# Convolution taps moved into the first projection of a hybrid diffusion trunk on Trainium2

## What is computed

```python
def _conv_module(u2, p):
    a, b = jnp.split(u2, 2, axis=-1)
    u = a * jax.nn.sigmoid(b)
    y = lax.conv_general_dilated(u, p['conv_w'][:, None, :].astype(u.dtype), window_strides=(1,),
                                 padding=((CONV_WIDTH // 2, CONV_WIDTH // 2),),
                                 dimension_numbers=('NWC', 'WIO', 'NWC'), feature_group_count=CONV_DIM)
    y = jax.nn.silu(_layer_norm(y + p['conv_b'], p['conv_ln_g'], p['conv_ln_b']))
    return y @ p['w_conv_out']
...
def _mixing(h, p, kv_ctx):
    ...
    u2, q, k, v, f, g = jnp.split(h @ p['w_in'], SPLITS, axis=-1)
    ...
    conv_out = _conv_module(u2, p)
    ...
    merged = gates[:, :, 0] * conv_out + gates[:, :, 1] * attn_out + gates[:, :, 2] * fnet_out
    return merged @ p['w_out'], k, v
```

## Time and profile before

| | |
|---|---|
| median of 3 runs | 1402.83 us (1402.35 to 1403.17) |
| the profiled execution | 1399.74 us, of which the span of the trace is 1397.9 us |
| PE busy | 1262.8 us (90%) |
| DVE busy | 914.3 us (65%) |
| ACT busy | 619.3 us (44%) |
| POOL busy | 300.6 us (22%) |
| attention's first scores on PE | 311.49 us from the span's start |

### The profile page before, as it was taken

One profiled execution on the slowest core, in us unless ns is written; L12 is line 12 of the kernel. 1 busy time (PEld: TensorE's weight loads), 2 busy tenths in 40 slices (PEclk: granted clock), 3 DMA queues, 4 the chain that ended last, 5 costly groups with the idle time before them and its releaser, 6 DMA issues.

```text
span 1397.9 us, 18848 instructions
## 1 busy us (share of the span) xinstructions
PE 1262.8 (90%) x7338; PEld 1009.5 (72%) x7338; DVE 914.3 (65%) x1070; ACT 619.3 (44%) x693; POOL 300.6 (22%) x199
## 2 busy tenths in 40 slices
PE   2899979997999999999798459999999999999992
PEld 1688769985888999999797436666666666666661
DVE  1501656779766233613745549999999999999993
ACT  2421122221433222231212237777777777777772
POOL 1051000000332222233221402222222222222212
PEclk9899989997999999999998569999999999999996
DMA  9764651321110111235202969999999999999964
GB/s 282 247 211 151 226 91 61 106 70 60 44 48 28 43 53 60 90 104 199 63 31 109 380 214 352 379 378 378 380 381 378 380 381 382 381 381 381 381 232 160
DMA packets 156070, 302.54 MB, mean 216 GB/s; under 512 B 6984, under 2 KB 60707, under 8 KB 155758
## 3 DMA queue, kind: packets, MB, share of 16 engines
q1 hardware_dynamic: 144268, 267.63, 53.4%
q10 hardware_dynamic: 7986, 21.66, 4.2%
q0 software_dynamic: 3760, 12.45, 4.2%
HBM read 286.63 MB, written 15.08 MB: 216 GB/s over the span
## 4 chain that ended last, share of the span: by engine, by line
PE 82%; DVE 10%; ACT 2%; DMA 2%; issue 2%; SPq 1%; POOL 0%; ACTq 0%; POOLq 0%; DVEq 0%
PE bank L1287 16%; PE bank L1288 15%; PE bank L1289 15%; PE bank L1310 5%; PE bank L1311 4%; PE bank L1312 4%; PE bank L1313 4%; PE bank L1314 4%; PE bank L1315 4%; DVE fa L913 2%; PE bank L1516 1%; PE bank L1589 1%; PE bank L1342 1%; PE bank L1489 1%; DMA mask<-const_mask 1%
## 5 line engine op out<-in xcount | busy, mean ns | idle before, releaser
L1219 DVE TENSOR_TENSOR l2r<-w,h2r 128x2048 fp32r<-128x2048 f32 x189 | 431.6, 2290 | 55.2 <-ACT h2r L820 53.5
L820 ACT CAST h2r<-w 128x2048 fp32r<-128x2048 f32 x192 | 367.1, 1913 | 132.0 <-PE bank L1289 128.1
L1287 PE MATMUL bank<-h2r,xTh 128*80 128x512 f32 x512 | 203.4, 397 | 1.0 <-DVE xTl L1225 1.0
L1288 PE MATMUL bank<-l2r,xTh 128*80 128x512 f32 x512 | 202.1, 395 | 0.0
L1289 PE MATMUL bank<-h2r,xTl 128*80 128x512 f32 x512 | 200.6, 392 | 0.0
L495 POOL TENSOR_TENSOR half<-half 1x1 f32<-1x1 f32 x32 | 67.6, 2112 | 369.2 <-DVE ye L1263 367.9
L441 POOL TENSOR_TENSOR lring<-wring,hring 128x2048 fp32r<-128x2048 f32 x21 | 96.9, 4614 | 196.9 <-ACT hring L536 196.9
L1310 PE MATMUL bank<-hTh,hring 128*128 128x320 f32 x320 | 107.0, 334 | 3.3 <-DVE hTl L974 3.3
L1289 PEld LDWEIGHTS bank<-h2r,xTl 128*80 128x80 f32 x512 | 76.2, 149 | 43.1 <-issue 0.9
L1287 PEld LDWEIGHTS bank<-h2r,xTh 128*80 128x80 f32 x512 | 76.2, 149 | 42.6 <-DVE xTl L1225 1.3
L1288 PEld LDWEIGHTS bank<-l2r,xTh 128*80 128x80 f32 x512 | 76.3, 149 | 39.8 <-issue 0.7
(11 more groups left out here) (276 smaller groups left out, 2455.8 us busy)
## 6 DMA issues: line engine op xcount, KB each, us to landing
w<-in_w_e_gate SPq DMA_DIRECT2D x64, 1024.0 KB, 12.0
w<-in_w_e_up SPq DMA_DIRECT2D x64, 1024.0 KB, 12.7
w<-in_w_e_down SPq DMA_DIRECT2D x64, 1024.0 KB, 12.2
wring<-in_w_in SPq DMA_DIRECT2D x21, 1024.0 KB, 5.2
fa<-in_w_ada SPq DMA_DIRECT2D x13, 1024.0 KB, 7.4
wring<-in_w_ada SPq DMA_DIRECT2D x11, 1024.0 KB, 7.6
wring<-in_w_out SPq DMA_DIRECT2D x4, 1024.0 KB, 5.3
fa<-in_w_in SPq DMA_DIRECT2D x3, 1024.0 KB, 5.1
```

The source lines that it names most:

```text
L820: act.copy(h2r[:, k % 3, :], w2[:, k, :]).then_inc(e_hi, 1)
L1219: dve.tensor_tensor(l2r[:, k % 3, :], w2[:, k, :], h2r[:, k % 3, :].bitcast(F32), ALU.subtract).then_inc(e_lo, 1)
L1287: pe.matmul(out, lh, rh, start=start, stop=False)
L1288: pe.matmul(out, lh, rl, start=False, stop=False)
```

## The change

- The `u2` blocks run in the order 0, 4, 1, 5, 2, 6, 3, 7, so that after every second block one channel block of `U` is complete. The units `in 1` and `in 2` change places in `UNITS`.
- After every `u2` block but the first, DVE issues six taps, of the channel blocks that are complete. `conv` now picks the block with the fewest taps; each tap waits for the previous one of its own block.
- In the `f` loop the groups of taps are 6, 4, 4, 6 (4 each before), in the `uv` loop 6 (4 before), behind the seven low parts 7 (11 before) until none is left, in attention none.
- The low part of `in 2`, the first gate unit, is made by DVE and not by POOL, ahead of the loop.
- Raw slot 4 moves from `fa` 13492 to 2560, so both waits on it go (`s_turn` on SP, `s_lop` on DVE). `h3`/`l3` move to the place of `uvh`/`uvl`, and their old place becomes a fourth pair `h4`/`l4`, which `in 8` uses.

```diff
-for _i, _n in enumerate((1, 2, 3, 10, 11)):
+for _i, _n in enumerate((2, 1, 3, 10, 11)):
...
-LOW_BY_DVE = [("in", 0), ("dft", 0), ("dft", 1)] + [("in", i) for i in (8, 9, 4, 5, 6, 7, 20, 21)]
+LOW_BY_DVE = [("in", 0), ("in", 2), ("dft", 0), ("dft", 1)] + [("in", i) for i in (8, 9, 4, 5, 6, 7, 20, 21)]
...
-JOBS += [("u2", i) for i in range(8)]
+U2_ORDER = [0, 4, 1, 5, 2, 6, 3, 7]
+JOBS += [("u2", i) for i in U2_ORDER]
...
-        raw_slots = [wring[:, 0, :], wring[:, 1, :], fa[:, 8704:8704 + UN], fa[:, 6656:6656 + UN], fa[:, 13492:13492 + UN]]
+        raw_slots = [wring[:, 0, :], wring[:, 1, :], fa[:, 8704:8704 + UN], fa[:, 6656:6656 + UN], fa[:, 2560:2560 + UN]]
...
-        H_SLOT = {u: n % 3 if n < 9 else (n + 1) % 2 for n, u in enumerate(SPLITS)}
+        H_SLOT = {u: n % 3 if n < 8 else 3 if n == 8 else (n + 1) % 2 for n, u in enumerate(SPLITS)}
...
-                elif SLOT[u] == 4:
-                    sp.wait_ge(s_turn, 1)
...
-            behind = {0: ("in", 2), 1: ("in", 3), 3: ("in", 10), 5: ("in", 11)}
-            for b in range(8):
+            behind = {0: ("in", 1), 2: ("in", 3), 3: ("in", 10), 6: ("in", 11)}
+            for p, b in enumerate(U2_ORDER):
...
+            def conv(n, ready=CB):
 
                 for _ in range(n):
-                    if tap[0] == len(taps):
+                    c = min(range(ready), key=lambda x: len(taps[x]))
+                    k = len(taps[c])
+                    if k == CW:
                         return
...
-                        dve.wait_ge(s_cv, tap[0] - CB + 1)
+                        dve.wait_ge(s_cv, taps[c][-1])
...
-            for b in range(8):
-                rows_out(8 + b)
-                if b >= 1:
-                    ada_mod(7 + b)
+            lo(U_OF[("in", 2)])
+            for p, b in enumerate(U2_ORDER):
+                rows_out(8 + p)
+                if p >= 1:
+                    ada_mod(7 + p)
                 if b >= 4:
+                    c = b - 4
                     dve.wait_ge(s_ja, freed(J_OF[("u2", b)])[1])
...
                     ins.then_inc(s_u, 1)
+                    dve.wait_ge(s_u, c + 1)
+                if p >= 1:
+                    conv(6, (p + 1) // 2)
...
-                if i == 0:
-                    dve.wait_ge(s_lop, lo_count("pool", FIVE))
                 rows_out(17 + 2 * i)
...
-                conv(4)
+                conv(4 if i in (1, 2) else 6)
...
                 uv_lo(g)
-                conv(4)
+                conv(6)
 
             for i in (9, 4, 5, 6, 7, 20, 21):
                 lo(U_OF[("in", i)])
-                conv(11)
+                conv(7)
...
-                conv(2)
                 if it < len(ITEMS):
```

More of the change, by code:

```diff
@@ L200, in trunk @@
                 uvl = place(t2, "uvl", [P, 2, TT, 256], F32R)
+            with ExitStack() as t2:
+                h3 = place(t2, "h3", [P, UN], F32R)
+                l3 = place(t2, "l3", [P, UN], F32R)
             xg_f = place(p1, "xg_f", [P, TT * D])
@@ L203, in trunk @@
                 place(t3, "before", [P, 2560])
-                h3 = place(t3, "h3", [P, UN], F32R)
-                l3 = place(t3, "l3", [P, UN], F32R)
+                h4 = place(t3, "h4", [P, UN], F32R)
+                l4 = place(t3, "l4", [P, UN], F32R)
             fa = place(p1, "fa", [P, 17648])
@@ L332, in trunk @@
         FIVE = U_OF[("in", 11)] + 1
-        raw_slots = [wring[:, 0, :], wring[:, 1, :], fa[:, 8704:8704 + UN], fa[:, 6656:6656 + UN], fa[:, 13492:13492 + UN]]
+        raw_slots = [wring[:, 0, :], wring[:, 1, :], fa[:, 8704:8704 + UN], fa[:, 6656:6656 + UN], fa[:, 2560:2560 + UN]]
         SLOT = [u % 5 if u < FIVE else (u - FIVE + 2) % 4 if u < EARLY else u % 2 for u in range(N_U)]
-        H_SLOT = {u: n % 3 if n < 9 else (n + 1) % 2 for n, u in enumerate(SPLITS)}
+        H_SLOT = {u: n % 3 if n < 8 else 3 if n == 8 else (n + 1) % 2 for n, u in enumerate(SPLITS)}
         def split(u):
             k = H_SLOT[u]
-            return (h3[:, :], l3[:, :]) if k == 2 else (hring[:, k, :], lring[:, k, :])
+            if k < 2:
+                return hring[:, k, :], lring[:, k, :]
+            return (h3[:, :], l3[:, :]) if k == 2 else (h4[:, :], l4[:, :])
         def raw(u):
@@ L565, in _ @@
                 act.copy(hTh[:, dc, :], xT[:, dc, :]).then_inc(s_hh, 1)
-            hi(U_OF[("in", 1)])
+            hi(U_OF[("in", 2)])
             def mod_store(k):
@@ L587, in _ @@
                     take(n, tmp5[:, b % 2, :], ACT.Tanh, 0.5).then_inc(s_ja, 1)
-                if b >= 2:
-                    mod_store(b - 2)
-                if b in behind:
-                    hi(U_OF[behind[b]])
+                if p >= 2:
+                    mod_store(p - 2)
+                if p in behind:
+                    hi(U_OF[behind[p]])
             act.wait_ge(s_u, 4)
@@ L898, in lo @@
                                   ALU.subtract).then_inc(s_lov, 1)
-            taps = [(k, c) for k in range(CW) for c in range(CB)]
-            tap = [0]
-            def conv(n):
+            taps = [[] for c in range(CB)]
+            n_taps = [0]
+            def conv(n, ready=CB):
                 for _ in range(n):
-                    if tap[0] == len(taps):
+                    c = min(range(ready), key=lambda x: len(taps[x]))
+                    k = len(taps[c])
+                    if k == CW:
                         return
-                    k, c = taps[tap[0]]
                     if k == 0:
@@ L915, in conv @@
                     ins.then_inc(s_cv, 1)
-                    tap[0] += 1
+                    n_taps[0] += 1
+                    taps[c].append(n_taps[0])
             def rows_out(i):
@@ L1062, in _ @@
                         dve.tensor_copy(dst, bank[7][r0:r0 + DH, 0:P]).then_inc(s_at, 1)
-            conv(len(taps))
+            conv(CB * CW)
             def split_lo(src, n0):
@@ L1083, in _ @@
                 product("fnet", b)
-            dve.wait_ge(s_cv, len(taps))
+            dve.wait_ge(s_cv, CB * CW)
             for c in range(CB):
@@ L1395, in _ @@
                 run(steps)
-                ada(8 + b)
-                if b >= 1:
-                    ada_sum(7 + b)
+                ada(8 + p)
+                if p >= 1:
+                    ada_sum(7 + p)
             for b in range(4):
```

4 lines of the change are left out of this document (2 added, 2 removed).

## The result

| | us |
|---|---|
| before, median of 18 runs | 1401.43 (1395.00 to 1403.17, and one run of 6904.56) |
| the change, median of 18 runs | 1392.01 (1384.99 to 1396.31) |
| ratio | 0.9936, 95% interval 0.9921 to 0.9952 |
| forecast | 1395.4, range 1392.0 to 1399.4 |

By the ratio the change saves 9.0 us (6.7 to 11.1); the forecast's sum was 7.4 us. The median lies 3.4 us under the predicted time: 1.4 us of that is that before itself came out at 1401.43 beside it and not at 1402.83, the rest, 2.0 us, is a saving larger than forecast. The single long run of before moves neither the median nor the ratio.

What follows compares the result with a forecast made beforehand. PE, busy 90% of the span, was taken as the bound. Terms -10.2 + 1.2 + 1.6 = -7.4 us against the profiled 1399.74 gave 1392.3; adding the median's 3.1 gave 1395.4 us, range 1392.0 to 1399.4.

Steps and rivals of the forecast that it cites:

- Attention's start: PE's 8.12 us wait for DVE's scaling and a further 1.0 us go, plus 1.1 from the clock: 10.2 us gained.
- The part for the clock: At attention's start, PE fed without a break gets its full clock back some 2 us after 316.6: net 1.1 us gained.
- The second block of u2: PE waits there for DVE's low part of `in 2`: a loss of 1.2 us, with no fall of the clock.
- The end of f: DVE's last group grows from four to six taps, all on PE's path: 1.6 us lost, upper bound 1.6 + 1.7.
- The constants: Two 1 MB loads issued some 13 us earlier could delay the constants in flight: 0 to 1 us.
- The taps in u2: 42 taps behind seven u2 blocks fit in DVE's idle time, so they cost PE nothing.
- at 1.386 a group of six takes 8.3 us: In u2 beside POOL, taps at the longest single time exceed a block's DVE idle time by 0.5 to 1.4 us.
- Costed at nothing: Side effects without cost: PE's block order, POOL's later low parts (`in 11` by 17 us), slot 4's move, other taps.
- The first: Another wait replaces the one removed at attention's start: only 4.5 us gained, 1398.3 us; chance 0.13.
- The second: The clock falls at u2's new wait and the half clock at `uv` lasts longer: 3.8 us lost, 1399.2; chance 0.10.
- The third: The u2 taps cost DVE more than a block has, PE stands some 16 us in u2 and f: 1411; chance 0.06.
- The fourth: The wait at attention's start is hidden anyway, by the cast and k's copies, leaving only losses: 1405.6 us; chance 0.03.

Runs made afterwards that it cites:

- e1: The change's block order, slots and `in 2` low part, but with before's tap groups (none in u2, two in each of attention's first ten items): 1401.02 us, ratio 0.9989.
- e8: The change with 19 taps taken out of u2's last groups and put back in attention's first ten items: 1396.76 us, ratio 0.9984.
- e4: The change with ACT's cast of `in 2` moved earlier and its low part given back to POOL: 1397.36 us, ratio 0.9956.
- e11: The change itself, measured again on the same chip as e9 and e10: 1391.36 us, ratio 0.9933.
- e7: The change with nine taps behind each u2 block and not six: 1407.54 us, ratio 1.0071.
- e3: Before, with its old order, slots and splits and only the taps regrouped into f, `uv` and behind low parts, none in attention: 1388.42 us, ratio 0.9899.
- e9: The change's block order and moved slots with the tap groups of e3, none in u2 or attention: 1388.15 us, ratio 0.9914.
- e2: The change with tap groups of 6, 6, 6, 0 in the f loop, so none at f's end: 1391.9 us, ratio 0.9926.
- e10: e3 once more, on the same chip as e9 and e11: 1387.8 us, ratio 0.9912.
- e6: The change with the low parts of `in 3`, `in 10` and `in 11` made by DVE and not POOL: 1391.51 us, ratio 0.9934.
- e5: The change with SP's wait for the transposes put back ahead of slot 4's first load: 1392.53 us, ratio 0.9948.

## Why the prediction was right, and which step was not

- **Attention's start: 10.2 us forecast, 9.71 in the traces.** From item 0 to item 10 before took 37.36 us, with PE busy for 28.22: 9.14 idle (the 8.12, and 1.02 for the 1.0 of the forecast). The change has 0.00 idle, as forecast. The part for the clock, 1.1 us, was over-sized: I had the clock rise at some 318.6, some 2 us behind the first transposes, for which I had no row, and it rose at 323.1. The sign that I gave, a half clock of some 7 us, failed with it: it is 10.2 us. PE did 9.65 us of work at the lower level, before 9.29: nothing was won there. What is left is 0.57 us. The clock fell at 312.9, in a wait of 1.71 us ahead of item 0 that every kernel here has, so in this trace taking the 8.12 us away did not keep it up. The first latent item starts 8.84 us earlier against the transposes of k, over the 7 that I had asked for. e1 and e8 show that it is the taps' leaving that brings this term.
- **The second block of u2: 1.2 forecast**, a wait of 1.13 and 1.20 in the table. The clock stayed at 1.00, and e4 shows that the wait is the low part's.
- **The end of f: 1.6 forecast, 1.62 measured** in the wait. The half clock behind it was shorter in the change than before (10.3 and 13.8 us) and longer in e11 (17.1), but with 11.51 us of PE's work in it against 10.90 before, so the upper bound was not reached.
- **The constants: 0 to 1 forecast.** 1.25 between the two traces, but 5 us between executions of like kernels, so the term can't be read from one trace each. The two loads were issued 8.9 and 3.2 us earlier (at 19.11 and 25.27, before at 28.02 and 28.43), and not some 13.
- **The taps in u2, costed at nothing: the sum is right, the step is not.** The step that failed is "at 1.386 a group of six takes 8.3 us". A group beside a low part takes 10.04. I took the longest tap for a slower rate; it was one blockade, as long as what is left of POOL's instruction, and the other five taps keep their 0.90 us. So the sign "up to 1.4 beside POOL" failed too, with 5.37. Then "DVE falls behind by some 3 us at most" had to fail as well: in u2 DVE has 56.17 us of work in 67.80, where I had some 9.2 + 42 x 0.92 = 48. The term was still near nothing (0.22 us), as the cover I named, DVE's idle time and the slack of one block, was large enough. That it was is partly luck, since I had costed the meetings at 3 us and they are 12.7; it is not much larger, as e7 shows.
- **The sum: 7.4 forecast, 9.0 (6.7 to 11.1) measured.** With the measured sizes the four terms give -9.71 + 1.20 + 0.22 + 1.62 = -6.7. That is the edge of the measured interval. The other 2.3 us aren't settled. They are no term of the list; stretches of half clock, which vary by execution (the one at `uv` alone differs by some 3 us between the change and e11), are my guess, and no run here isolates them.
- **Costed at nothing.** The low part of `in 11` came 11.1 us later (127.22, before 116.12) and not 17, and nothing waited for it, as forecast.
- **The rivals.** The first (another wait in its place) did not come: PE has none in ten items. The second neither: at u2 the clock stayed whole, and at `uv` the longest stretch of the change (e11) costs 0.3 us more than before's. The third is real but not at six taps a block. The fourth is excluded by the 9.14 us of idle time that went.

e3 and e9 also show what I had not asked: whether u2 was the place for the taps at all. DVE had idle time in `uv` and behind the low parts, and regrouping the taps there brings 14 us with no new order.

## To carry to other kernels

Where filler work holds up an in-order engine just ahead of a stage whose first result another engine waits for, count the filler there, and move it to stretches where this engine waits for a third; first by changing the numbers in the list, before the order of the main work is touched. Where, as here, a DVE instruction with two SBUF inputs meets a POOL `TENSOR_TENSOR` on SBUF, cost the one that comes second at the whole of what the first has left, once per meeting, and not at a slower rate; whether that matters is read from what DVE's next result releases. When executions of one kernel spread by more than a term is worth, compare traces from mark to mark, and leave the sum to the medians.

## What the runs showed of the hardware

- DVE and POOL on SBUF: a tap of 0.90 us that meets a low part of 4.64 takes up to 5.37, a product pair 4.67 instead of 0.87, and an instruction over 16 columns 2.62 instead of 0.17. A POOL instruction that begins while a tap runs is held up too: 5.35 us instead of 4.64 (e7), 1.43 instead of 0.73 (before). A `rows_out`, with one input in SBUF, keeps its 0.42 beside a low part. A DVE low part in POOL's stead takes 2.29.
- TensorE's clock: at attention's start, behind a wait of 1.71 us ahead of item 0 that all thirteen traces have, PE works at 1.2 GHz for a stretch that was 10.2 us in six of the traces (the change, e11, e2, e4, e9, e10), 17.1 in three (before, e6, e8), 3.4 in two (e5, e7) and 27.3 in e1; e3 had none. Behind a wait of 1.24 us late in attention it fell in one trace of the change and not in the other.
